# Modulation sums in PSUM and out of the first pairs, an earlier and interleaved input stage, and one more low part on POOL

## The reference

```
def adaln(cond, w, b):                       # two conds: c, c_ctx
    m = jax.nn.silu(cond) @ w + b            # w: (1024, 9 * 1024) per layer
    return m.reshape(cond.shape[0], 1, N_MOD, D_MODEL)
def modulate(x, g, shift, scale):
    return rmsnorm(x, g) * (1.0 + scale) + shift
def swiglu(x, wg, wu, wd):
    return (jax.nn.silu(x @ wg) * (x @ wu)) @ wd
def ffn_half(x, m, j, g, wg, wu, wd):
    return x + 0.5 * m[:, :, j + 2] * swiglu(modulate(x, g, m[:, :, j], m[:, :, j + 1]), wg, wu, wd)
```

## Time and profile before

| | us |
|---|---|
| median of 3 runs (lowest, highest) | 2727.3 (2726.56, 2728.72) |
| profiled execution, its own time | 2727.09 |
| its span on the core | 2725.6 |
| busy PE | 2568.2 (94%) |
| busy DVE | 1917.7 (70%) |
| busy ACT | 1064.7 (39%) |
| busy POOL | 1019.1 (37%) |
| mean granted TensorE clock | 0.98 of full |

### The profile page before, as it was taken

How to read it: one execution, slowest core, us unless ns; L and a number is a source line. 1 busy time by engine, 2 the same in 40 slices (tenths; PEclk the granted TensorE clock), 3 DMA queues, 4 the chain that set the end, 5 groups by cost and what they waited for, 6 DMA issues and landing times. The chain is left out here.

```text
span 2725.6 us, 43019 instructions
## 1 busy us (share of the span) xinstructions
PE 2568.2 (94%) x17283; PEld 2465.5 (90%) x17283; DVE 1917.7 (70%) x2907; ACT 1064.7 (39%) x1740; POOL 1019.1 (37%) x671
## 2 busy tenths in 40 slices
PE   6999999899989998999989899999999999899998
PEld 5999999899766998898989798999999999899998
DVE  6897798725677697778778877776564569756473
ACT  4221122243665553333335342424532555334343
POOL 3454455343200343424344342534442224442433
PEclk8999999999999999999999899999999999899999
DMA  7443543431100221424224133322321222122222
GB/s 275 151 134 120 175 144 110 138 105 49 57 1 1 93 93 62 138 65 139 78 95 138 47 113 105 113 89 86 96 63 55 66 82 93 47 93 78 78 74 74
DMA packets 205075, 259.88 MB, mean 95 GB/s; under 512 B 4965, under 2 KB 160233, under 8 KB 204905
## 3 DMA queue, kind: packets, MB, share of 16 engines
q1 hardware_dynamic: 204232, 254.88, 28.2%
q10 hardware_dynamic: 672, 2.62, 0.3%
HBM read 253.66 MB, written 3.82 MB: 94 GB/s over the span
## 5 line engine op out<-in xcount | busy, mean ns | idle before, releaser
L2469 POOL TENSOR_TENSOR wl<-raw,wh 128x512 fp32r<-128x512 f32 (+1 forms) x440 | 665.4, 1542 | 921.3 <-ACT wh L2582 856.6
L2582 ACT CAST wh<-raw 128x2048 fp32r<-128x2048 f32 (+2 forms) x122 | 210.6, 1726 | 549.4 <-PE psU L3326 427.4
L2897 DVE SCALAR_TENSOR_TENSOR macc<-mraw,cs,macc 128x512 f32<-128x512 f32 x448 | 396.4, 952 | 2.4 <-DMA mraw<-in_mod_w 2.4
L2519 POOL TENSOR_TENSOR wl<-raw,wh 128x512 fp32r<-128x512 f32 x54 | 84.0, 1556 | 458.7 <-ACT wh L2722 458.7
L3322 PE MATMUL psU<-hh,wh 128*128 128x386 f32 (+1 forms) x896 | 207.2, 312 | 2.7 <-issue 2.7
L3322 PE MATMUL psG<-hh,wh 128*128 128x386 f32 x880 | 206.7, 316 | 1.1 <-DVE hl L3293 1.1
L3326 PE MATMUL psU<-hh,wl 128*128 128x386 f32 (+1 forms) x896 | 206.0, 311 | 0.0
L3324 PE MATMUL psU<-hl,wh 128*128 128x386 f32 (+1 forms) x896 | 205.5, 310 | 0.0
L3326 PE MATMUL psG<-hh,wl 128*128 128x386 f32 x880 | 202.9, 312 | 0.0
L3324 PE MATMUL psG<-hl,wh 128*128 128x386 f32 x880 | 202.4, 311 | 0.0
L3322 PE MATMUL psG<-ah,wh 128*128 128x384 f32 (+1 forms) x560 | 135.0, 323 | 54.1 <-issue 29.5
(11 more groups left out here) (680 smaller groups left out, 7095.9 us busy)
## 6 DMA issues: line engine op xcount, KB each, us to landing
mraw<-in_mod_w SPq DMA_DIRECT2D x64, 1024.0 KB, 6.2
raw<-in_ffn_w_gate SPq DMA_DIRECT2D x44, 1024.0 KB, 5.2
raw<-in_ffn_w_up SPq DMA_DIRECT2D x44, 1024.0 KB, 5.1
raw<-in_ffn_w_down SPq DMA_DIRECT2D x44, 768.0 KB, 4.3
raw<-in_odd_w_in SPq DMA_DIRECT2D x12, 1024.0 KB, 5.1
raw<-in_even_w_in SPq DMA_DIRECT2D x9, 1024.0 KB, 5.1
raw<-in_ffn_w_down SPq DMA_DIRECT2D x6, 1024.0 KB, 6.6
raw<-in_ffn_w_down SPq DMA_DIRECT2D x8, 640.0 KB, 4.1
```

Source lines behind the costliest of these rows:

```text
L2469: ins = nc.gpsimd.tensor_tensor(wl[:, slot, piece], raw[:, slot, piece], wh[:, slot, piece].bitcast(F32), ALU.subtract)
L2519: nc.gpsimd.tensor_tensor(part3(f, wl, 5), quarter(n, 1, 1), part3(f, wh, 5).bitcast(F32), ALU.subtract).then_inc(block_plo, 1)
L2582: nc.scalar.copy(wh[:, slot, 0:width], raw[:, slot, 0:width]).then_inc(w_hi, 1)
L2897: ins = nc.vector.scalar_tensor_tensor(out=macc[:, c], in0=mraw[:, s, k], scalar=scalar, in1=macc[:, c], op0=ALU.mult, op1=ALU.add)
```

## The change

- `mod_sum` adds in the PSUM banks psA and psB, one for each condition; only the last step of the second half writes `macc` in SBUF. It can be issued in slices of steps. Its first step waits until the reduce before has read psA.
- `mod_turn` is eight matmuls with the blocks of `macc` as weights and a column of ones, which put the eight sums of a pair into eight columns of psA; `mod_reduce` is then one small addition.
- `MOD_PLAN` takes the modulation out of the head pairs of ffn1 to ffn3. In ffn1 and ffn2 one pair of units goes with the six units of each part, two steps at a time at two places in the units j = 1 to 4; the turn follows the last unit. The down parts carry two pairs (three of the parts) or one pair (three parts): the first pair's halves stand before the residuals of i = 0 and i = 1 and PE turns it after tile (1, 1); the second pair's halves stand behind the residuals of i = 2 and i = 3 and PE turns it after tile (3, 1).
- In the head, all eight `input_rows`, `input_high`, the four input sums and POOL's low parts of the input go with the first pair. The sums lie in the place of `mraw`, and SP waits for their low parts before it loads modulation again.
- In the short down part each `input_sum_lo` is followed by a residual, and the weight sums of the first unit stand between the other residuals.
- POOL, not DVE, makes the low part of the first weight sum (`low_first_sum`).

The diff, cut, in the order of the file: the plan, the place of the sums, SP, POOL, ACT, DVE (`mod_sum`, a unit, the short down part, a down part), PE.

```diff
-MOD_PLAN = {0: (12, 6, 10, 6), 1: (4, 0, 4, 4, 2), 2: (4, 0, 4, 4, 0), 3: (4, 0, 0, 0, 0)}
+MOD_PLAN = {0: (12, 6, 10, 6), 1: (2, 4, 2, 4, 2, 2), 2: (2, 4, 2, 2, 2, 2), 3: (0, 0, 0, 0, 0, 0)}
...
+    sum_m, _ = view("sum_m", [P, 3, QUAD], at_m, end_m)
+    sum_f = [sum_m[:, 0], sum_m[:, 1], sum_m[:, 2], zf[:, 0, 1]]
...
+                    if j == 1 and plan[2 * part - 2]:
+                        if part == 1:
+                            sp.wait_ge(sum_lo, 4 * f)
+                        for s in range(2):
+                            modulation(2 * part - 2, 0, s)
...
+            def low_first_sum(part, j):
+                pool.wait_ge(block_hi, 5 * seven_index(f, part, j) + 3)
+                nc.gpsimd.tensor_tensor(part1(f, wl, 3), part1(f, wsum, 3), part1(f, wh, 3).bitcast(F32),
+                                        ALU.subtract).then_inc(block_plo, 1)
...
+                if i == 0:
+                    pool.wait_ge(zh_ok, DT * f)
+                    pool.wait_ge(sum_ok, 4 * f)
+                    for kh, h in ((0, 0), (1, 0), (1, 1)):
+                        nc.gpsimd.tensor_tensor(zl[:, kh, h], zf[:, kh, h], zh[:, kh, h].bitcast(F32),
+                                                ALU.subtract).then_inc(zl_ok, 1)
...
-                for k in range(4 * i, 4 * i + 4):
-                    input_high(k)
+                if i == 0:
+                    for k in range(DT):
+                        input_high(k)
...
+        def mod_sum(q0, i, s, first=0, last=MOD_STEPS):
+            if first == 0:
+                dve.wait_ge((mred_ok, macc_ok)[s], (i * 2) + (q0 + s))
+                dve.wait_ge(mod_in[s], (i * 16) + ((q0 - MOD_HEAD) // 2 * 16 + 16))
+            for step in range(first, last):
+                k, c = step // 2, step % 2
+                acc = (psA, psB)[c][:]
+                ...
+                out = macc[:, c] if s == 1 and k == MOD_K - 1 else acc
+                ins = nc.vector.scalar_tensor_tensor(out=out, in0=mraw[:, s, k], scalar=scalar, in1=acc, op0=ALU.mult, op1=ALU.add)
...
                 if more:
                     first_low(part, j + 1)
                     first_sums(part, j + 1)
+                unit_mods(part, 4 * j)
                 dve.wait_ge(seven_mm, 7 * u + 5)
...
-                    sum_lows(part, j + 1, 3)
...
                 if more:
                     sum_lows(part, j + 1, 4)
+                unit_mods(part, 4 * j + 2)
+            def unit_mods(part, step):
+                step -= MOD_STEPS // 2
+                if plan[2 * part - 2] and 0 <= step < 2 * MOD_STEPS:
+                    mod_sum(MOD_BASE[f, 2 * part - 2], 0, step // MOD_STEPS, step % MOD_STEPS, step % MOD_STEPS + 2)
...
             for s in range(4):
-                input_sum(s)
-                residual(s // 2, s % 2, rb)
-            for s in range(4):
                 input_sum_lo(s)
+                residual(s // 2, s % 2, rb)
...
                 for i in range(4):
+                    if i < 2 and mods:
+                        mod_sum(q0, 0, i)
                     for m in range(2):
                         residual(i, m, rb)
+                        if i == 2 and m == 0 and mods:
+                            mod_reduce(q0)
+                    if i >= 2 and mods > 2:
+                        mod_sum(q0, 1, i - 2)
...
-                    ins = turn((psA, psB)[c][:, t * P:(t + 1) * P], macc[:, c, t * P:(t + 1) * P])
+                    ins = nc.tensor.matmul(psA[:, 4 * c + t:4 * c + t + 1], macc[:, c, t * P:(t + 1) * P], one, start=True, stop=True)
...
-                pe.wait_ge(block_lo, 4 * u + 3)
+                pe.wait_ge(block_plo, 2 * u + 1)
                 seven(ps, 2, 3, sum_h[:, 0], sum_l[:, 0], True)
...
+                if plan[2 * part - 2]:
+                    mod_turn(MOD_BASE[f, 2 * part - 2])
-                        if m == 0 and i and 2 * (i - 1) < mods:
-                            mod_turn(MOD_BASE[f, 1 + part], i - 1)
+                        if m == 1 and i % 2 and i - 1 < mods:
+                            mod_turn(MOD_BASE[f, 2 * part - 1], i // 2)
```

More of the change, by code:

```diff
@@ L2421, in down @@
                               w_down[:, k0:k0 + PART_TILES, f, i * PAIR:(i + 1) * PAIR])
-                mods = plan[1 + part]
+                mods = plan[2 * part - 1]
                 for i in range(4):
                     down(i)
-                    if i >= 1 and 2 * (i - 1) < mods:
+                    if i == 1 and mods:
                         for s in range(2):
-                            modulation(1 + part, i - 1, s)
+                            modulation(2 * part - 1, 0, s)
+                    if i >= 2 and mods > 2:
+                        modulation(2 * part - 1, 1, i - 2)
         for name in phases:
@@ L2532, in seven_ffn @@
                     product_lo(FT * f + 2 * i + m, m, 2 * i + m)
+                if i == 0:
[4 more added lines that the diff above has]
+                                                ALU.subtract).then_inc(zl_ok, 1)
             split_lo(down_unit(f, 0, 1), (base + 1) % 2)
[L2534 to L2537, removed]
+            low_first_sum(1, 0)
             low_last_quarter(1, 0)
@@ L2544, in seven_ffn @@
                     if j < 2 * PART_PAIRS - 1:
+                        low_first_sum(part, j + 1)
                         low_last_quarter(part, j + 1)
@@ L2553, in seven_ffn @@
                 if part < N_PARTS:
+                    low_first_sum(part + 1, 0)
                     low_last_quarter(part + 1, 0)
@@ L2883, in _ @@
         st = Steps(dve, dve_steps)
[L2885 to L2902, removed]
+        def mod_sum(q0, i, s, first=0, last=MOD_STEPS):
[4 more added lines that the diff above has]
+                k, c = step // 2, step % 2
+                scalar = cs[:, s * MOD_K + k, c:c + 1]
+                acc = (psA, psB)[c][:]
+                if s == 0 and k == 0:
+                    st.mark(nc.vector.tensor_scalar(acc, mraw[:, s, k], scalar, None, ALU.mult))
+                    continue
+                if k:
+                    st.wait(back=1)
+                out = macc[:, c] if s == 1 and k == MOD_K - 1 else acc
+                ins = nc.vector.scalar_tensor_tensor(out=out, in0=mraw[:, s, k], scalar=scalar, in1=acc, op0=ALU.mult, op1=ALU.add)
+                if step == MOD_STEPS - 1:
+                    ins.then_inc(macc_ok, 1)
+                else:
+                    st.mark(ins)
         def mod_reduce(q0, i=0):
@@ L2907, in mod_reduce @@
             col = bass.ds(i * 4 + 2 * q0, 4)
[L2908 to L2914, removed]
+            nc.vector.tensor_tensor(mod[:, :, col], psA[:, 0:8].rearrange("p (c t) -> p c t", c=2),
                                     modb[:, col].rearrange("p (o t) -> p o t", o=1).to_broadcast([P, 2, 4]),
@@ L3167, in seven_ffn @@
                     ins.then_inc(g_scaled, 1)
-                for k in range(4 * i, 4 * i + 4):
-                    input_rows(k)
-                if carries:
-                    mod_sum(MOD_BASE[f, 0], i, 1)
+                if i == 0:
+                    for k in range(DT):
+                        input_rows(k)
                 dve.wait_ge(a_lo, FT * f + 2 * i)
@@ L3185, in seven_ffn @@
                     ins.then_inc(prod_ok, 1)
-                if carries:
-                    mod_reduce(MOD_BASE[f, 0], i)
+                if i == 0:
+                    dve.wait_ge(zh_ok, DT * f)
+                    for s in range(4):
+                        input_sum(s)
             rb = res_base[f, 0]
             gate_of(l * N_MOD + (2 if j2 == 0 else 8), 0.5, rb)
-            dve.wait_ge(zh_ok, DT * f)
-            dve.wait_ge(up_mm, old_tiles(f) + HEAD_TILES)
-            for s in range(4):
-                input_sum(s)
-                residual(s // 2, s % 2, rb)
             for s in range(4):
                 input_sum_lo(s)
+                residual(s // 2, s % 2, rb)
             first_low(1, 0)
```

63 lines of the change are left out of this document (25 added, 38 removed).

## The result

The changed kernel takes 2734.98 us at the median, against 2726.93 us of the kernel before measured beside it: 1.0031 times as long, with a 95% interval of 1.0022 to 1.0040. So it is slower by 8 us, where 5.4 had been forecast and a time of 2732. The profiled execution has a span of 2734.0 us and a granted clock of 0.978.

What follows compares the result with a forecast made beforehand. PE, busy 94% of 2725.6 us, was taken as the bound, with the units a chain over four engines. Terms 14.4 − 2 − 27 − 2 + 21 + 1 = +5.4 on 2727.1 gave 2732 us, range 2709 to 2752.

Steps and rivals of the forecast that it cites:

- three signs of being wrong: Turns under 1.2 us (−9), units not longer (−21), or heads losing less than 20 us.
- ffn0, 14 turns without a wait: In ffn0, each turn lengthens by 1.03 us, paid in full in 14 turns where PE does not wait: +14.4 us.
- ffn0, last part: Ffn0's last three turns wait for DVE; two reduces fall away, the turn grows by 1.03: about −0.65 each, −2 us.
- three heads: Two turns gone from each head, idle PE from 14.5 to 7.2 us: −8.9 each, −27 us for three.
- down parts of ffn1, ffn2: Six down parts take 318.6 us for 320.44, waits for sums moved to the end, not removed: −2 us (±5).
- units of ffn1, ffn2: DVE's steps lengthen the change from up to gate unit by 1.75 us in 12 places: +21 us.
- units of ffn3: Without modulation, six up-to-gate changes keep only low 3's exchange for a POOL part: +1 us (0 to 6).
- The step with the cast: Head: ACT's later cast of the second pair's up weights delays POOL; PE waits 4, then 1.5 and 1.7 us.
- A: Rival: the units absorb the steps, low 4's contention goes, places cost 0.65 us; 2719 us, chance 0.15.
- B: Rival: POOL is not late in the head, so heads give −42 us; 2717 us, chance 0.13.
- C: Rival: POOL's new part takes the shared port first at up-to-gate changes, 2.85 us a place; 2750 us, chance 0.20.
- D: Rival: a modulation step into PSUM takes 65 ns longer than one in SBUF, +4.7; 2737 us, chance 0.10.

Runs made afterwards that it cites:

- the earlier cast: The changed kernel with ACT casting the second pair's up weights in the first head pair behind four input tiles, not all eight: 2725.15 us, 0.9986 of the kernel before.

## Why the prediction was right

The time lies 3 us from the forecast one and inside its range, and none of the prediction's three signs of being wrong appeared: turns take 1.7 us, the gate units are longer, the heads lose 30. The mechanisms are those that were named, with one left out almost everywhere, the granted clock. That the sum is off by only 3 us is partly luck: the terms below miss by 17 us in all, in both directions.

| term | forecast | measured in the profiles |
|---|---|---|
| ffn0, 14 turns without a wait | +14.4 | +12.1 |
| ffn0, last part | −2 | +3.7 |
| three heads | −27 | −30.0 |
| down parts of ffn1, ffn2 | −2 | −3.2 |
| units of ffn1, ffn2 | +21 | +24.0 |
| units of ffn3 | +1 | +0.3 |
| the rest of the kernel | 0 | +1.4 |
| sum | +5.4 | +8.3 |

The measured terms are differences of the two profiles' stretches (the spans, 2734.0 and 2725.6, differ by 8.4).

**The turn.** Right in mechanism and size: it is longer by 0.92 us, not 1.03, since one column costs 0.107 us a record here for 0.114 in the earlier trace rows. That ffn0's 14 turns are paid on PE was shown by putting the old one back.

**The last part of ffn0** has the wrong sign, and a step is missing there. The stretch in both kernels, before first:

```profile
455.47:543.37 87.90, 77.15 (x508) 76.11 (x506) 67.10 (x112) 23.02 (x31) 36.29 (x28) 0.96 0.43 144
```

```profile
467.83:559.47 91.64, 84.67 (x531) 83.63 (x530) 63.26 (x101) 22.32 (x31) 35.05 (x28) 0.91 0.43 140
```

Idle PE shrinks from 10.75 to 6.97 us, as the lost reduces should make it, and more. But PE's busy time grows by 7.5 us, of which the three longer turns are 2.8; the rest goes with a granted clock of 0.91 for 0.96. The forecast counted the waits and left out the clock behind them: 17.1 us of the stretch run at 0.50, where 6.8 did, though no wait is longer than 2.0 us and before there were three of 2.2 to 2.9 for sums. With the old turn put back the stretch still takes 90.48 us, at 0.94, so the new turn is not all of it; why the clock falls more often stays open.

**The heads.** The step with the cast was right in place and nearly in size: 4 us were forecast for the up weights and 1.5 + 1.7 for the short down part's weights and `al`; there are 2.85, and 3.3 together. These are what was described (the earlier cast moved the first into the second), with POOL 1 us less late at the up weights. A third wait, 1.83, was not foreseen: a residual queued behind a weight sum that itself waits for PE. So idle PE falls by 6.5 us a head where 7.3 were forecast, and with two turns less (1.6) that makes 24.4 us for the three. The other 5.6 were not worked out: they go with the granted clock, 0.96, 1.00 and 1.00 where the heads had 0.95, 0.93 and 0.93.

**The down parts.** With two pairs the account is right: 7.18 us of wait for 7.7, and half clock behind it. That clock costs 1.7 us in the turn and 0.9 to 2.3 in the first gate unit of the next part (13.72 to 15.16 us for 12.81 or 12.82), about 3.5 together for the forecast 2.8. The longest of these units:

```profile
1195.59:1210.75 15.16, 15.16 (x86) 15.16 (x86) 7.06 (x10) 4.87 (x9) 2.56 (x2) 0.80 0.29 96
```

The table counts these units with the units, 5.4 us in all, so its row of the down parts looks better than the forecast was. The parts with one pair take 148.0 us for 143. In two of them, the last of their phases, the turn waits 2.3 us for its sums, a wait that the forecast put at nothing, since DVE does the next norm's work ahead of the second half:

```profile
1410.34:1460.07 49.73, 47.46 (x321) 47.20 (x320) 39.37 (x61) 17.62 (x26) 22.24 (x16) 0.97 0.30 96
1893.84:1946.45 52.61, 47.62 (x321) 47.12 (x320) 41.41 (x66) 20.12 (x29) 22.22 (x16) 0.96 0.32 102
```

With the 5.4 us back where the forecast had them, the down parts are +2.2 for −2 and the units +18.6 for +21.

**The units.** The sum was right, the account of it only in part. At the 12 changes the cost is 1.32 us a place for 1.75, 15.9 together; nearly all of the other 8 lie in first gate units, slowed by the clock behind the last turn's wait or the residual's. And the mechanism was told as one chain with no slack, where the experiments show more than one: moving the steps off that chain, within the gate unit, gained 0.07 us a unit; taking them out of the gate units brought these to 12.31, with 12.50 for the up unit that does them. DVE, busy 12.5 of 13.78 us there, is the engine that these chains share.

**The rivals.** A fell by place (1.32 is above its 0.65), though its argument, that low 4 loses its contention, holds in the rows above (0.68 for 1.79 in the earlier trace rows); the low part of the second sum took it up, 1.52 us for 0.69, beside `low_first_sum`, and the last sum still takes 1.34 (1.41 before). B fell: POOL was late. C's condition came true, for POOL starts `low_first_sum` at 1084.40 and DVE low 4 only at 1088.02, but its price did not: a place costs 1.32, not 2.85, and without POOL's part the kernel is slower. D fell: the step's rows (ns, min/median/max) are

```profile
L2917 DVE SCALAR_TENSOR_TENSOR psA<-mraw,cs,psA x192: 742/748/755, 57.1 to 1916.2; 128x512 f32<-128x512 f32 x192
...
L2917 DVE SCALAR_TENSOR_TENSOR macc<-mraw,cs,psA x32: 731/741/748, 66.6 to 1917.6; 128x512 f32<-128x512 f32 x32
```

Before, with the sum in SBUF:

```profile
L2897 DVE SCALAR_TENSOR_TENSOR macc<-mraw,cs,macc x448: 733/741/2057, 51.8 to 2310.4; 128x512 f32<-128x512 f32 x150
```

The median was 741 ns; it is 7 ns longer in PSUM, not 65, and the longest of 192 is 755. The fixed costs that the Trainium skill's "VectorE: DVE Perf Modes" gives in its section on the TRN2 errata don't show in this pair of operations. Where the sums did gain is that POOL no longer stretches them: before, the longest took 2057 ns. The Trainium skill's "SBUF — State Buffer", under "Who interferes with whom", says that a VectorE instruction with at most one input in SBUF, outside the two-port modes, does not contend with GpSimd, and that one with two contends with a GpSimd instruction that reads SBUF. The rows agree on both sides, with at most 2057 ns against 755.

## What to carry to other kernels

Cheap work for a side engine is only cheap where that engine has room: count its busy time and its waits unit by unit (here the up units took four steps and the gate units didn't), and put the work where it prepares nothing. A transfer from a side engine to TensorE, here two reduces of 0.68 us on DVE for 0.9 us of matmuls, costs in full where TensorE has no gap. For each wait, count its own length and the clock of what runs behind it.

## What had not been expected of the hardware

That eight one-column matmuls take 1.71 us, more than twice the 0.79 of eight transposes of 128 columns, had been forecast from the earlier trace rows. What the clock does behind a wait had not. The same idle time of 2.05 us was followed by full clock in one gate unit and by a stretch at the lower level in another (1.00 and 0.89 over the units). Idle times of 1.18 us left the clock at 1.00 in all twelve places. A shorter wait than 2.05 us can be followed by half clock when the new turn stands behind it: in ffn0's last part the first wait for a sum is 1.34 us in the changed kernel and 1.33 us with the old turn put back. The turn and what follows, first with the new turn, then with the old one:

```profile
499.61 1.94 PE L3367 MATMUL psA<-consts,macc 128*128 128x1 f32 x16 [1.34 <-DVE macc L2917]
```

```profile
502.00:505.41 3.41, 3.41 (x15) 3.41 (x14) 3.31 (x4) 0.00 (x0) 1.50 (x2) 0.50 0.17 36
```

```profile
486.59 0.65 PE L3339 MATMUL psA<-ident,macc 128*128 128x128 f32 x4 [1.33 <-DVE macc L2917]
```

```profile
486.59:500.00 13.41, 11.98 (x82) 11.71 (x83) 10.51 (x17) 1.89 (x4) 3.23 (x3) 1.00 0.38 130
```

This is one pair of cases; that the turn is the cause is not shown by it.
